# Order of the two chunks' work inside a slot of a chunked delta-rule scan

## The reference

```
decay = jnp.exp(-jnp.exp(heads(w)))

def step(S, inp):
    r_t, d_t, k_t, v_t, kk_t, a_t = inp
    sa = jnp.einsum('bhij,bhj->bhi', S, -kk_t)
    S = (S * d_t[:, :, None, :] + sa[..., None] * (kk_t * a_t)[:, :, None, :]
         + v_t[..., None] * k_t[:, :, None, :])
    return S, jnp.einsum('bhij,bhj->bhi', S, r_t)

s_new, ys = lax.scan(step, s0, seq)
```

## Time and profile before

| | |
|---|---|
| time, median of 3 runs | 2927.4 us (2923.29 to 2931.53) |
| the profiled execution's own time | 2937.65 us |
| its span | 2935.5 us |
| PE busy | 2659.1 us, 91% |
| DVE busy | 1174.7 us, 40% |
| ACT busy | 796.9 us, 27% |
| mean granted PE clock | 0.945 |
| the scan over the prompt | about 343 to 599 us of the span |

### The profile page before, as it was taken

The page is one execution under the profiler, slowest core; times in us unless marked ns, Lnnn a source line. Parts: engine busy times, 40 slices in busy tenths (PEclk is TensorE's granted clock), DMA queues, the critical chain, the costliest instruction groups (busy, mean ns, idle before and its releaser), DMA issues. The chain is left out here.

```text
span 2935.5 us, 48987 instructions
## 1 busy us (share of the span) xinstructions
PE 2659.1 (91%) x21514; PEld 2381.2 (81%) x21514; DVE 1174.7 (40%) x2020; ACT 796.9 (27%) x1246; POOL 180.5 (6%) x215
## 2 busy tenths in 40 slices
PE   5799599977996899968799999998799999999998
PEld 4798398956994556534799999997689999999998
DVE  4533666534234566526313233452452222222223
ACT  3221422221123344423212121222332221222221
POOL 1000233203001000011000000000000000000000
PEclk7899799988997899988899999998999999999999
DMA  5620100035220000067411112403111111111111
GB/s 170 226 59 17 17 4 4 4 105 117 83 59 21 1 1 1 1 228 285 156 51 47 44 46 55 124 8 110 48 37 51 44 50 44 51 44 46 49 44 67
DMA packets 178932, 192.08 MB, mean 65 GB/s; under 512 B 18214, under 2 KB 162897, under 8 KB 173624
## 3 DMA queue, kind: packets, MB, share of 16 engines
q1 hardware_dynamic: 168665, 127.05, 14.7%
q0 software_dynamic: 9888, 61.87, 6.0%
q10 hardware_dynamic: 168, 0.04, 0.0%
HBM read 165.28 MB, written 28.00 MB: 66 GB/s over the span
## 5 line engine op out<-in xcount | busy, mean ns | idle before, releaser
L3436 PE MATMUL ps<-ff_hidden_high,ff_high 128*128 128x352 f32 x768 | 247.7, 323 | 0.0
L3437 PE MATMUL ps<-ff_hidden_low,ff_high 128*128 128x352 f32 x768 | 246.7, 321 | 0.0
L3438 PE MATMUL ps<-ff_hidden_high,ff_low 128*128 128x352 f32 x768 | 246.4, 321 | 0.0
L586 PE MATMUL ps<-xf_h,ff_high 128*128 128x352 f32 x720 | 232.3, 323 | 2.1 <-DVE ff_low L575 2.1
L587 PE MATMUL ps<-xf_l,ff_high 128*128 128x352 f32 x720 | 230.8, 321 | 0.0
L588 PE MATMUL ps<-xf_h,ff_low 128*128 128x352 f32 x720 | 230.7, 320 | 0.0
L3036 PE MATMUL ps<-xn_h,me_gate_w_high 128*128 128x352 f32 x576 | 186.6, 324 | 4.9 <-DVE me_gate_w_low L3102 4.9
L3037 PE MATMUL ps<-xn_l,me_gate_w_high 128*128 128x352 f32 x576 | 185.3, 322 | 0.0
L3038 PE MATMUL ps<-xn_h,me_gate_w_low 128*128 128x352 f32 x576 | 185.1, 321 | 0.0
L3545 DVE TENSOR_TENSOR x<-x,ps 128x1056 f32<-128x1056 f32 x64 | 80.3, 1254 | 224.8 <-PE ps L3438 224.8
L3539 DVE TENSOR_TENSOR ff_hidden_low<-ff_act,ff_hidden_high 128x1056 fp32r<-128x1056 f32 x32 | 40.3, 1258 | 307.0 <-ACT ff_hidden_high L3511 307.0
(11 more groups left out here) (708 smaller groups left out, 6409.3 us busy)
## 6 DMA issues: line engine op xcount, KB each, us to landing
ff_raw<-in_w_ff SPq DMA_DIRECT2D x64, 512.0 KB, 4.0
me_gate_w_raw<-in_w_in SPq DMA_DIRECT2D x23, 512.0 KB
pj_raw<-in_w_in SPq DMA_DIRECT2D x13, 512.0 KB, 4.2
xn_high<-xn_h POOLq DMA_DIRECT2D x1, 4224.0 KB, 12.1
xn_low<-xn_l POOLq DMA_DIRECT2D x1, 4224.0 KB, 24.2
xn_h<-xn_high POOLq DMA_DIRECT2D x1, 4224.0 KB, 15.8
xn_l<-xn_low POOLq DMA_DIRECT2D x1, 4224.0 KB, 26.2
xn_h<-xn_high SPq DMA_DIRECT2D x1, 4224.0 KB, 13.0
```

The lines of the kernel that those rows point to most:

```text
L586: e.matmul(o, W.hi[:, z, k, :], rh[:, k, n], start=k == ks[0], stop=False)
L3436: e.matmul(o, W.hi[:, u % NSPL, 2 * k + z, :], hh[:, r, ns], start=k == 0, stop=False)
L3437: e.matmul(o, W.hi[:, u % NSPL, 2 * k + z, :], hl[:, r, ns], start=False, stop=False)
L3438: mm = e.matmul(o, W.lo[:, u % NSPL, 2 * k + z, :], hh[:, r, ns], start=False, stop=k == GB - 1)
```

## The change

In every slot the order within each pair of late and early work is turned round, on PE, DVE and ACT: the level 3 half of the older chunk now comes ahead of the level 0 half of the younger one, and the level 4 half ahead of the level 1 half; the same for steps, copies and updates. On PE, `rhs(s-1)`, which follows `late_step(s-1, 3)`, now also stands ahead of `early_step(s, 0)`. The third early level of the slot keeps its place. No instruction is added or left out, and none changes its operands.

The core of the diff (PE, then DVE; ACT has the same exchange in its copies):

```diff
@@ PE
+                if late:
+                    late_half(s - 1, 3)
                 if early:
                     early_half(s, 0)
-                if late:
-                    late_half(s - 1, 3)
                 if begin:
                     turn_operands(s + 1)
-                if early:
-                    early_step(s, 0)
                 if late:
                     late_step(s - 1, 3)
                     rhs(s - 1)
+                if early:
+                    early_step(s, 0)
                 if begin:
                     if s >= 0:
                         e.wait_ge(s_mk, s + 1)
                     scores(s + 1, Bt, s_sb)
+                if late:
+                    late_half(s - 1, 4)
                 if early:
                     early_half(s, 1)
-                if late:
-                    late_half(s - 1, 4)
                 if begin:
                     turn_values(s + 1)
+                if late:
+                    late_step(s - 1, 4)
                 if early:
                     early_step(s, 1)
-                if late:
-                    late_step(s - 1, 4)
@@ DVE
+                if late:
+                    late_update(s - 1, 3)
                 if early:
                     early_update(s, 0)
-                if late:
-                    late_update(s - 1, 3)
                 if begin:
                     mask_scores(s + 1, MR, s_sb, s_mb)
                 if ahead is not None:
                     exponents(ahead)
                 if ready is not None:
                     operands(ready)
+                if late:
+                    late_update(s - 1, 4)
                 if early:
                     early_update(s, 1)
-                if late:
-                    late_update(s - 1, 4)
```

More of the change, by code:

```diff
@@ L1401, in _ @@
                 early, late, begin = 0 <= s < NCH, s >= 1, s + 1 < NCH
+                if late:
+                    late_copy(s - 1, 3)
                 if early:
                     early_copy(s, 0)
-                if late:
-                    late_copy(s - 1, 3)
                 if begin:
@@ L1409, in _ @@
                     copy_rhs(s - 1)
+                if late:
+                    late_copy(s - 1, 4)
                 if early:
                     early_copy(s, 1)
-                if late:
-                    late_copy(s - 1, 4)
                 if begin:
```

## The result

The changed kernel takes 2947.73 us (four runs) against 2928.38 us for the kernel before (four runs): ratio 1.0067, 95% interval 1.0050 to 1.0085. A second set gave 2945.08 against 2931.49 us, ratio 1.0054 (1.0037 to 1.0070). It is slower by 0.5 to 0.7%, not by the forecast 0.2%, and outside the range. The profiled execution took 2946.73 us, span 2944.5 us.

What follows compares the result with a forecast made beforehand. PE bounds the kernel; in slots 1 to 12 it waits for DVE's early update. Slots 1 to 12, 13 and 14, 15 and slot 1's start: 4.0 + 0.5 + 1.0 + 0.5 = 6.0 us, giving 2933.4 us; range 2926.5 to 2941.

Steps and rivals of the forecast that it cites:

- the slots' clock stays at 1.00: Scan slots: sign named for the profile after, PE's granted clock not falling; no cost for falls in the sum.
- the start of slot 1: Late half now first, waiting until 362.05; the early half's eight multiplications follow instead of filling the wait: +0.5 us, at most 1.0.
- 12 x 0.33 = 4.0 us: Slots 1 to 12: DVE's late level 4 update ahead of the early one delays it, and PE, 0.33 us per slot.
- Slots 13 and 14, 0.23 us each: No preparation there; early update starts 0.47 us later, so PE's third half can start 0.23 us later: 0.5 us together.
- Slot 15, +1.0 us: Early level 0 update moves behind the late work, so the early step of level 1 starts at 583.71 instead of 582.71.
- Rival (a): Even slots: clock falls behind the gap grown to 2.02 us, 1.7 us each, 10.2 us if all six; chance 0.10.
- The argument against, that PE is busy on both sides of the gap: Even slots: reason given against clock falls there, beside PE having waited longer in slot 0, where the clock fell.
- The sign that it named for being wrong: Even slots: a clock fall there was listed among the observations that would show the forecast wrong.
- Rival (b): Behind the scan: clock falls from 610 to 650 us do not come, saving 9.1 us, 2924.3 us in all; chance 0.08.
- Rival (c): Slots 1 to 12: third half held by something that doesn't move, delay hidden, 2.0 us left, 2929.4 us; chance 0.10.
- 12 x 0.42 = 5.0 us: Slots 1 to 12: the skill's fp32 tensor_tensor duration taken as distance of starts; set aside for the measured 0.33 us.

Runs made afterwards that it cites:

- e1_back: Changed kernel, but in slots 1 to 12 DVE does the early level 1 update before the late level 4 one, as before; ratio 1.0014 to the kernel before.
- e4_odd: Kernel before, with DVE alone doing the late level 4 update ahead of the early level 1 one in odd slots 1 to 11; ratio 1.0007.
- e5_first: Kernel before, with only the first pair (levels 3 and 0) exchanged on PE, ACT and DVE; ratio 1.0022.
- e6_second: Kernel before, with only the second pair (levels 4 and 1) exchanged on PE and ACT, DVE as before; ratio 1.0013.
- e10_oddgap: Kernel before, with DVE doing the last instruction of exponents twice in slots 1 to 11, lengthening the odd slots' PE gap; ratio 1.0038.

## Why the prediction was wrong

Its bound, the way in which the delay enters and the size of the delay held. The step that failed is the one that it put at nothing: that *"the slots' clock stays at 1.00"* behind a gap of 2.02 us. The runs showed four falls there, 5.9 us of the 13.0. A second term was too small: the start of slot 1, 0.5 us in the sum, took 1.8.

- *"12 x 0.33 = 4.0 us"* was right: odd and even slots each lengthened by 0.33 us, and the exchange on DVE alone in the odd slots cost 2.0 us for six.
- *Slots 13 and 14, 0.23 us each:* they cost 0.13 each. The third half does wait for its update there, as predicted (in slot 14 583.21 + 0.69 = 583.90 us, the half begins at 583.95); why the slot grows by less is not shown.
- *Slot 15, +1.0 us:* 1.0 (24.5 us from the last L1286 to the end before, 25.5 after).
- *Start of slot 1, +0.5 us:* 1.8 us. The wait grew by 0.76 us, inside the bound of 1.0, but this stretch was already at half clock, and with PE standing still for longer the clock came back later; that made the other 1.1 us, which the step did not price. The kernel that undid only this exchange in slot 1 got both parts back, together.
- So without falls in slots 2 to 12 the sum is 4.0 + 0.3 + 1.0 + 1.8 = 7.1 us, where 6.0 was forecast.
- *Rival (a), with a chance of 0.10, came true in four of six slots.* It was priced at 1.7 us a fall; the slots show 1.5 (17.80 - 16.27 in the one above). The four together make 5.9 us, and 7.1 + 5.9 = 13.0 us, the whole difference. The step that failed is the weighing: rows existed for a gap of 1.69 us without a fall and of 2.5 us with one, and the forecast put 2.02 us on the first side without a reason. The argument against, that PE is busy on both sides of the gap, was no argument: it was so in every fall in slots 2 to 12. The sign that it named for being wrong, a fall of the clock in even slots, is the one that came.
- *Rival (b)* did not come in either profile: behind the scan the clock fell for 24 us in one piece, as before, now from 620 us on. *Rival (c)* fell with the gaps of 1.37 and 2.02 us.
- Two readings of rows were off without an effect on the sum. What the prediction and the earlier trace rows call slots 6 and 7 are slots 7 and 8: `exponents` is only in odd slots and `operands` only in even ones. And the preparation takes 3.6 and 4.2 us (461.72 to 465.28 and 477.01 to 481.21), or 4.2 and 4.8 with the mask in front of it, not 4 to 5.
- The range ended at 2941 us. The scan's 13.0 us on the 2927.4 us of the first three runs would be 2940.4 us, just inside. But over 30 later runs the median of the kernel before was 2931.5 us (2920.74 to 2938.23), and on that it is 2944.5 us. The forecast took 2 us of spread for a median of three runs, which is too little. The measured 2947.73 us lies above either.

The term from the Trainium skill (VectorE: DVE Perf Modes, section on the TRN2 errata), 12 x 0.42 = 5.0 us, would have been further off for the slots than the row's 0.33.

## What to carry to other kernels

A delay that only lengthens an idle gap of PE can have two prices: its own length, and the clock. When the new gap lies between one behind which the trace shows a fall and one behind which it shows none, nothing on record says on which side it is, so price the fall as likely; here it was worth more than the delay itself. And before reordering work around a gap, look at what stands in front of the waited-for instruction on its engine: here the preparation could stand in DVE's idle time at the slot's start, or be freed from POOL's company, for 16 to 20 us.

## What the runs showed that was not expected

DVE instructions with two SBUF operands took markedly longer while POOL ran one: L1266 to L1268 took 1.21 to 1.22 us beside POOL's masks and 0.68 to 0.69 us without them, and the four L1252 took 2.50 us against 0.89 us at the slot's start. Updates that read PSUM took 0.68 or 0.69 us in both cases. The Trainium skill has the rule (SBUF — State Buffer, section "SBUF: two separate sides"): a DVE instruction with two SBUF inputs and a GpSimd instruction that reads SBUF share a port pair, and one of them blocks; which one it is goes by who starts first. The trace agrees: in the kernel before L1265 started first (477.01) and took 0.68 us as ever, while POOL's L1430 (477.17) took 1.10 us instead of the 0.73 that it takes elsewhere. By the kernel in which only POOL was held back it cost this scan 15.9 us, with what the clock takes in slots 0 and 1.

A gap of PE of 2.0 to 2.2 us in otherwise dense work lowered the clock in 18 of the 30 places in which the profiles of five kernels (the changed one, the exchanges in all and in even slots, slot 1 undone, and the longer odd gap) have one; the second profile of the changed kernel repeats the first. One of 1.5 to 1.7 us never did, in 36 places of six profiles (before, e1_back, e4_odd, e5_first, e6_second and the even slots of e10_oddgap).
